# RWKV scan in residual form: values and corrections in opposite partition halves, level tiles by VectorE, keys turned by chunk

## The reference, cut to what matters

```python
def step(s, inp):
    w_t, a_t, k_t, v_t, kk_t = inp[:5]
    s = (s * w_t[:, :, None, :]
         - jnp.einsum('bhvk,bhk->bhv', s, kk_t)[..., None] * (kk_t * a_t)[:, :, None, :]
         + v_t[..., None] * k_t[:, :, None, :])
    y = jnp.einsum('bhvk,bhk->bhv', s, inp[5]) if emit else None
    return s, y
```

## Time and profile before

| what | value |
|---|---|
| median of 3 runs | 4092.16 us (4091.16, 4092.16, 4100.14) |
| span of the profiled execution | 4085.5 us, 6.7 us under the median |
| TensorE busy | 3690.0 us, 90% of the span |
| VectorE, ScalarE, GpSimd busy | 2226.9, 1064.1, 491.0 us |
| one scan stage (four of them) | 86 to 86.5 us |
| one prep stage (four of them) | 57.5 to 61.5 us |

### The profile page before, as it was taken

The page is one execution under the profiler, slowest core; times in us unless marked ns, Lnnn a source line. Parts: engine busy times, 40 slices in busy tenths (PEclk is TensorE's granted clock), DMA queues, the critical chain, the costliest instruction groups (busy, mean ns, idle before and its releaser), DMA issues. The chain is left out here.

```text
span 4085.5 us, 66177 instructions
## 1 busy us (share of the span) xinstructions
PE 3690.0 (90%) x27408; PEld 2046.7 (50%) x27408; DVE 2226.9 (55%) x3700; ACT 1064.1 (26%) x2366; POOL 491.0 (12%) x675
## 2 busy tenths in 40 slices
PE   7899999687896899999998899997697968999998
PEld 4555665476643333333334655664586533333333
DVE  3554324688756544444443554335778667655654
ACT  3442110634311111111112542113444211111121
POOL 1100000221210111111111200000232110010100
PEclk9899999688998999999999899998798989999999
DMA  7200120200276577788873000211100336999996
GB/s 264 94 1 11 60 75 0 90 3 19 70 296 234 182 267 267 268 273 273 269 254 99 32 1 11 73 56 58 33 10 13 120 133 245 336 326 335 319 332 200
DMA packets 293592, 613.14 MB, mean 150 GB/s; under 512 B 37640, under 2 KB 50184, under 8 KB 286640
## 3 DMA queue, kind: packets, MB, share of 16 engines
q1 hardware_dynamic: 272752, 542.32, 37.2%
q0 software_dynamic: 20544, 66.60, 6.3%
HBM read 561.07 MB, written 47.79 MB: 149 GB/s over the span
## 5 line engine op out<-in xcount | busy, mean ns | idle before, releaser
L3017 PE MATMUL ps<-moe_w,e_hT 128*128 128x512 f32 x1024 | 449.4, 596 | 21.5 <-issue 8.9
L3148 DVE TENSOR_TENSOR moe_w<-moe_w 128x2048 f32<-128x2048 f32 x128 | 287.2, 2286 | 200.5 <-PE ps L2947 157.2
L2917 PE MATMUL ps<-moe_w,e_xs 128*64 128x512 f32 x1536 | 348.6, 596 | 0.8 <-DVE moe_w L3148 0.8
L2917 PE MATMUL ps<-moe_w,e_xT 128*64 128x512 f32 x1536 | 340.6, 592 | 0.8 <-DVE moe_w L3148 0.8
L3017 PEld LDWEIGHTS ps<-moe_w,e_hT 128*128 128x128 f32 x1024 | 192.3, 190 | 258.4 <-issue 255.6
L3154 DVE TENSOR_TENSOR e_cb<-e_part,ps 128x512 f32<-128x512 f32 x128 | 87.9, 686 | 335.1 <-ACT e_part L3056 249.3
L2917 PEld LDWEIGHTS ps<-moe_w,e_xT 128*64 128x64 f32 x1536 | 110.7, 137 | 218.7 <-issue 218.7
L2917 PEld LDWEIGHTS ps<-moe_w,e_xs 128*64 128x64 f32 x1536 | 105.3, 137 | 193.8 <-issue 192.3
L1197 PE MATMUL ps<-M 96*128 96x512 f32 (+1 forms) x400 | 183.2, 544 | 2.9 <-PEq L748 2.1
L3056 ACT COPY e_part<-ps 128x512 f32<-128x512 f32 x96 | 56.3, 586 | 480.7 <-PE ps L2917 472.4
L1057 PE MATMUL ps<-yT,hT 128*128 128x272 f32 (+1 forms) x608 | 148.1, 399 | 1.6 <-DMA yT<-in_w_in_dram 1.6
(11 more groups left out here) (420 smaller groups left out, 7163.9 us busy)
## 6 DMA issues: line engine op xcount, KB each, us to landing
moe_w<-in_w_gate_dram SPq DMA_DIRECT2D x128, 1024.0 KB, 14.1
moe_w<-in_w_up_dram SPq DMA_DIRECT2D x128, 1024.0 KB, 14.2
moe_w<-in_w_down_dram SPq DMA_DIRECT2D x128, 1024.0 KB, 13.2
m_mod_w<-in_w_ada_dram SPq DMA_DIRECT2D x24, 1024.0 KB, 6.6
o_mod_w<-in_w_ada_dram SPq DMA_DIRECT2D x24, 1024.0 KB, 7.6
yT<-in_w_in_dram SPq DMA_DIRECT2D x6, 2048.0 KB, 7.8
r_z<-z_rows SPq DMA_DIRECT2D x20, 512.0 KB, 3.3
z_rows<-p_zo POOLq DMA_DIRECT2D x36, 256.0 KB, 2.3
```

Source lines behind the costliest of these rows:

```text
L2917: ins = nc.tensor.matmul(ps[HF * q:HF * q + HF, b, :], x[:, k], weights[q][:, k], start=(first and k == 0), stop=(k == 3), skip_group_chec ...
L3017: ins = nc.tensor.matmul(ps[:, YB + c, :], hT2[:, 4 * half + k], quarter(name, e)[:, k], start=(half == 0 and k == 0), stop=(half == 1 and ...
L3148: nc.vector.tensor_tensor(to, a, b, ALU.subtract).then_inc(*td.up())
```

## The change

What it does, by part:

- **Operands.** `BK` is laid out by chunk, with 64 columns of padding at both ends that GpSimd zeroes. `by_token` now makes, for each tile, 14 transposes that read 64 partitions each and write 64 columns, for both directions at once. A chunk's key tile holds in one partition half the keys for the correction and in the other those for the value, and the values lie in the half in which the corrections don't. ScalarE copies a tile with three instructions (10 tiles, 30 copies), two tiles deep.
- **Residual form.** `W1`, `W2`, `MV`, `U`, `Se`, and `m_v`, `w1_w2`, `decayed` are gone. The carry of a chunk is now: `carry_r` on TensorE (masked products times values plus scaled queries `KE` times state), a negated ScalarE copy to `RR`, `carry_u` on TensorE (the inverse times `RR`), two ScalarE copies of 64x64 that put the correction beside the values, `carry_s` on TensorE with matmuls that contract over all 128 partitions, and VectorE's update of `S` from PSUM in one instruction.
- **Products.** They are issued in two groups of eight for both directions; the second group waits until the first is done. Each of the matmuls signals.
- **Level tiles.** VectorE writes both levels of `NL` straight from PSUM with one instruction (`level_rows`), then `UM` with three instead of four tiles per chunk; `level_x` waits for both. GpSimd makes `KE` instead.
- **T three deep.** Block rows are written up to two steps ahead. The next step's products wait for the last level of `TS`.

The diff, cut to its core (scan, then prep):

```diff
-                def products(d, s):
-                    if s:
-                        pe.wait_ge(*we[d].at(s))
...
+                def products(s, first):
+
+                    for d in DD:
+                        if first and s:
+                            pe.wait_ge(*ts[d].at(s * NLV))
+                        elif not first:
+                            pe.wait_ge(*p0[d].at(4 * s + 4))
+                    for c in range(2):
+                        for h in range(2):
+                            for d in DD:
+                                a = d if first else 1 - d
+                                out = ps[HALF[h if a else 1 - h], LV[d] + c, 0:4 * CH].rearrange("p (b n) -> p b n", n=CH)[:, a:3 + h:2 + h - a]
+                                nc.tensor.matmul(out, BK[d][HALF[h], 2 * order[d][s] + c, a], KR[d][HALF[h], :, toks(d, s, c)], start=True, stop=True) \
+                                    .then_inc(*(p0 if first else p1)[d].up())
...
+                def carry_r(d, s, q):
+                    n, c = 2 * s + q, chunks[d][q]
+                    if q == 0:
+                        pe.wait_ge(*kd[d].at(s + 1))
+                    pe.wait_ge(*su[d].at(n + 1))
+                    for h in range(2):
+                        nc.tensor.matmul(ps[HALF[1 - h], CA[d], Rc], UM[d][HALF[h], s % 2, c, 0], values(d, s, c, h)[HALF[h]], ...)
+                    for h in range(2):
+                        ins = nc.tensor.matmul(ps[HALF[1 - h], CA[d], Rc], KE[d][HALF[h], s % 2, 0, HALF[c]], S[d][HALF[h], n % 3], ...)
+                    ins.then_inc(*rm[d].up())
...
                 def carry_s(d, s, q):
                     n, c = 2 * s + q, chunks[d][q]
                     pe.wait_ge(*ue[d].at(n + 1))
+                    for h in range(2):
+                        ins = nc.tensor.matmul(ps[HALF[h], CA[d], Pc], keys(d, s, c, h), values(d, s, c, h), start=True, stop=True)
+                    ins.then_inc(*smm[d].up())
...
                 def level_x(d, s, v):
-                    pe.wait_ge(*nl[d].at(s * NLV + v + 1))
-                    pe.wait_ge(*ts[d].at(s * (NLV + 1) + v + 1))
+                    if v == 0:
+                        pe.wait_ge(*br[d].at(s + 1))
+                        pe.wait_ge(*nl[d].at(s + 1))
+                        pe.wait_ge(*um[d].at(s + 1))
+                    else:
+                        pe.wait_ge(*ts[d].at(s * NLV + v))
...
+                def level_rows(d, s):
+                    dve.wait_ge(*p1[d].at(4 * s + 4))
+                    nc.vector.tensor_tensor(NL[d][:], ps[:, LV[d]:LV[d] + 2, 0:CH].unsqueeze(1).broadcast_to([P, NLV, 2, CH]),
+                                            R["nlev"][:, d].unsqueeze(2).broadcast_to([P, NLV, 2, CH]), ALU.mult).then_inc(*nl[d].up())
...
+                def r_out(d, s, q):
+                    n = 2 * s + q
+                    act.wait_ge(*rm[d].at(n + 1))
+                    nc.scalar.activation(RR[d][:], ps[:, CA[d], Rc], ACT.Copy, scale=-1.0).then_inc(*re[d].up())
+
+                def u_out(d, s, q):
+                    n, c = 2 * s + q, chunks[d][q]
+                    act.wait_ge(*umm[d].at(n + 1))
+                    for h in range(2):
+                        ins = nc.scalar.copy(values(d, s, c, h)[HALF[1 - h]], ps[HALF[1 - h], CA[d], Uc])
+                    ins.then_inc(*ue[d].up())
```

```diff
-            for u, (d, t) in enumerate(units):
-                act.wait_ge(*turned.at(u + 1))
-                w = len(sources(d)) * P
-                nc.scalar.copy(BT[d][:, t].rearrange("p a n -> p (a n)"), ps[:, TBANKS[u % 4], 0:w]).then_inc(*tok_out.up())
+            for t in range(NT):
+                act.wait_ge(*turned.at(t + 1))
...
+                nc.scalar.copy(to[:, 2:4], two[:, :, 6 * CH:8 * CH].unsqueeze(2).broadcast_to([P, 2, 2, P])).then_inc(*tok_all.up())
+                nc.scalar.copy(to[:, 0:2], rows_[:, :, :, CH:3 * CH]).then_inc(*tok_all.up())
+                act.wait_ge(*tok_all.at(2 * t + 2))
+                nc.scalar.copy(to[CH:P, 0], rows_[CH:P, 0, :, 0:2 * CH]).then_inc(*tok_out.up())
```

More of the change, by code:

```diff
@@ L1680, in stage_rwkv_prep, with chunked @@
     allv, lnd, small = views(True), sg("ln_done"), sg("small_in")
-    turned, tok_out, ksd = sg("transposed"), sg("rw_tok"), sg("rw_ks")
-    BT, TBANKS = R["BYTOK"], (6, 3, 7, 4)
-    units = [(d, t) for t in range(NT) for d in range(2)]
-    def sources(d):
-        return (KR[d][:, 0], BK[d][:, 0], BK[d][:, 1]) + ((M[:, 4 + p],) if d == 0 else ())
+    turned, tok_all, tok_out, ksd = sg("transposed"), sg("rw_tok_all"), sg("rw_tok"), sg("rw_ks")
+    padded = sg("rw_padded")
+    BT, TBANKS = R["BYTOK"], ((3, 4), (6, 7))
+    HALF = [slice(0, CH), slice(CH, P)]
+    def chunked(a):
+        return a[:].rearrange("p (c n) -> p c n", n=CH)
     with nc.Block() as block:
@@ L1866, in _ @@
         def _(pool):
+            for d in range(2):
+                for e in (0, 2 * T + CH):
+                    ins = nc.gpsimd.memset(R["BKp"][d][:, e:e + CH], 0.0)
+            ins.then_inc(*padded.up())
             pool.wait_ge(*ed.at(2))
@@ L1931, in carry_u @@
+                    ins.then_inc(*umm[d].up())
+                    if has_y(d, s):
+                        if q == 0 and n_y(d, s):
                             pe.wait_ge(*ye[d].at(n_y(d, s)))
-                    for h in range(2):
-                        ins = nc.tensor.matmul(ps[HALF[c], CA[d] + h, Uc], W1[d][HALF[h], HALF[c]], S[d][HALF[h], n % 3],
-                                               start=True, stop=True, skip_group_check=True)
-                    if has_y(d, s):
+                        elif q == 1:
+                            pe.wait_ge(*ym[d].at(2 * n_y(d, s) + 1))
@@ L1944, in carry_s @@
                     pe.wait_ge(*ue[d].at(n + 1))
-                    for a, right in ((2, rows(d, s, 3)), (1, U[d])):
-                        if has_y(d, s):
-                            for h in range(2):
-                                nc.tensor.matmul(ps[HALF[h], CA[d] + c, Yc], right[HALF[c], HALF[h]], UM[d][HALF[c], s % 2, h, 2 * a - 1],
-                                                 start=False, stop=(a == 1), skip_group_check=True)
-                        for h in range(2):
-                            ins = nc.tensor.matmul(ps[HALF[h], CA[d] + c, Sc], rows(d, s, a)[HALF[c], HALF[h]], right[HALF[c], HALF[h]],
-                                                   start=(a == 2 and not has_y(d, s)), stop=(a == 1), skip_group_check=True)
@@ new lines, in level_x @@
+                def level_x(d, s, v):
+                    if v == 0:
[4 more added lines that the diff above has]
+                        pe.wait_ge(*ts[d].at(s * NLV + v))
+                    for c in range(2):
+                        for h in range(2):
+                            ins = nc.tensor.matmul(ps[HALF[h], LV[d], c * CH:(c + 1) * CH], NL[d][HALF[h], v, c], TS[d][HALF[h], s % 3, 0, c],
@@ L1971, in level_x @@
                                                    start=True, stop=True)
                     ins.then_inc(*xm[d].up())
-                def m_v(d, s):
-                    pe.wait_ge(*um[d].at(s + 1))
-                    for h in range(2):
-                        for c in range(2):
-                            ins = nc.tensor.matmul(ps[HALF[c], LV[d] + 1, HALF[h]], UM[d][HALF[c], s % 2, h, 2], rows(d, s, 3)[HALF[c], HALF[h]],
-                                                   start=True, stop=True)
-                    ins.then_inc(*mv[d].up())
@@ L2008, in _ @@
                         if car:
-                            w1_w2(d, s - 1)
+                            carry_r(d, s - 1, 0)
+                    if inv:
+                        products(s, True)
+                        products(s, False)
                     for d in DD:
-                        if inv:
-                            products(d, s)
                         if car:
@@ L2024, in _ @@
                             level_t(d, s, 0)
+                    for d in DD:
+                        if car:
+                            carry_r(d, s - 1, 1)
+                    for d in DD:
+                        if inv:
+                            level_x(d, s, 1)
                         if car:
                             carry_u(d, s - 1, 1)
-                    if inv:
-                        level_x(0, s, 1)
-                    if car:
-                        carry_s(0, s - 1, 1)
@@ L2031, in _ @@
-                    if inv:
-                        level_x(1, s, 1)
-                        level_t(0, s, 1)
-                    if car:
-                        carry_s(1, s - 1, 1)
-                    if inv:
-                        level_t(1, s, 1)
+                    for d in DD:
+                        if inv:
+                            level_t(d, s, 1)
+                    for d in DD:
+                        if car:
+                            carry_s(d, s - 1, 1)
             @block.vector
@@ L2115, in _ @@
```

(11 more changed lines are left out.)

258 lines of the change are left out of this document (126 added, 132 removed).

## The result

The changed kernel takes **4134.02 us** (median of 4 runs, 4129.59 to 4139.73) against 4091.66 us before (4 runs, 4090.03 to 4100.14): a ratio of 1.0099 with a 95% interval of 1.0077 to 1.012. It is 42 us slower. The prediction said 4110, 18 slower; its range, 4056 to 4134, ended where the measured time lies. The direction held, the size did not.

A forecast was written before the change was run, and what follows sets the result against it. It took the ring of waits within a step, not TensorE's load, as the bound: +0.49 us a step, +15.2 for four scans, +3 for prep, +18 on 4085.5, plus 6.7 to the median, 4110 us; range 4056 to 4134.

The forecast's parts named there:

- First step: First step of each scan, which has no carry: about 7.0 us against 7.80 before, -0.8.
- that the clock falls in the scans I give no case of its own: Clock in the scans: a fall through more idle time got no separate case or price.
- Piece 1: Step from products to `level_x`, direction 1: 3.3 us against 2.16 before, +1.15.
- The second waits for the first: Two groups of products at the step's start, in sequence: 0.67 + 0.06 + 0.67 = 1.40 us.
- Piece 2: Step from `level_x` to the end of the addition to T: 2.42 us against 2.40 before, 0.
- Piece 3: Step from the addition to the next products: 2.68 us against 3.36, -0.68, gained from `w1_w2` and its copies.
- The last carry: Scan's end, carry alone: 5.0 us against 4.8 before, +0.2.
- Prep: Stage ahead of each scan, ended by 30 ScalarE copies: +0.8 us each, +3 for four.
- TensorE's work as the bound: Rival for the scan step: fewer TensorE records make the kernel faster, 4040 or 4060 us; chance 0.25.
- The even case: Rival: product groups or correction copies overlap, step 7.75 to 8.05 us, kernel 4087 to 4098; chance 0.13.
- The third: Rival: 16 product signals a step and draining division changes add 0.3 and 0.4 us, kernel 4135; chance 0.12.
- The signs named beforehand: Scans 89 to 91 us, steps 8.4, TensorE under 85% busy; wrong if `level_x` starts within 2.8 us of products.

The follow-up runs named there:

- experiment 1: Changed kernel plus nine unused matmuls at the end of TensorE's part of every prep stage, keeping TensorE busy: 4117.6 us, ratio 1.0059.
- experiment 7: Kernel before the change, with only NL written by VectorE from PSUM and GpSimd's two level tiles gone: 4109.9 us, ratio 1.0052.
- experiment 10: Changed kernel with seven matmuls at prep's end, products waiting by chunk, carry_r between groups, mask by chunk, fewer signals, VectorE copying one prep tile: 4078.88 us.
- experiment 4: Changed kernel with the second group of products waiting by chunk, each half for the same half of the first group: 4114.58 us, ratio 1.0052.
- experiment 5: Changed kernel with carry_r issued between the two groups of products: 4124.51 us (4 runs), again 4115.84 us (6 runs).
- experiment 11: Changed kernel without ScalarE's third copy of each tile in prep, part of the computation thereby changed: 4131.07 us, ratio 1.0096.
- experiment 2: Kernel before the change, with the last ScalarE copy of every prep done four times: 4098.64 us, ratio 1.0013.
- experiments 8: Changed kernel with matmuls at prep's end, second product group waiting by chunk, carry_r between the groups and mask by chunk: 4089.89 us, ratio 0.9989.

## Why the prediction missed the size

- **First step, "about 7.0: -0.8".** It took 8.84 to 9.54 us. At full clock it takes 7.22 (experiment 1), so the layout was nearly right and the clock was wrong. This term and "that the clock falls in the scans I give no case of its own" are one error, worth 4 x 2.05 = 8 us in the profiled spans (+5.0 for -3.2): the fall of the clock was put at nothing, and it fell at all four entries. The rows I had the earlier trace rows showed a prep stretch and a scan at different clocks; I didn't ask what TensorE would be doing in the microseconds between them, although my own working let ScalarE's end move out by 0.8 us and its last transpose not. The idle time was in the numbers.
- **Piece 1, 3.3 us; it measured 3.56.** "The second waits for the first" was priced at a signal's hop of 0.06; it is 0.32, from 0.67 to 0.99. The mask's signal before `level_x` took 0.15 for 0.06 (885.98 to 886.13). Against that `carry_r` cost nothing after the first products. VectorE's four instructions were 1.68 for 1.70. Inside the piece I had also called the loss of GpSimd's tiles a gain, read from what sat between the mask and `level_x`; experiment 7 shows that in a full step of the old order it was none. That did not enter the sum.
- **Piece 2, 2.42 us; 2.61.** A change of division was taken at 0.09. `level_x`'s last record starts at 886.13 + 0.45 - 0.22 = 886.36, the next matmul at 886.51, which is the 0.09 over the usual 0.06. The carry of both directions took 0.61 for 0.55 and `level_t` to the end of the additions 1.62 for 1.55. The Trainium skill (TensorEngine Tiling (Array Packing), Key Properties) has the array drain on such a change; the trace agrees that there is a price, and it is less than half a record.
- **Piece 3, 2.68 us; 2.58.** `w1_w2`'s copies went, as forecast, though `carry_r` ahead of the products took 0.37 for 0.18.
- **The last carry, "took 4.8".** That was misread: the earlier trace rows give 5.00 (1080.56 to 1085.28 + 0.28). The ends of the scans, one step and the last carry each, came to +3.8 for 2.8 forecast.
- **Sum.** 8.75 for 8.41: 32 intervals at +25.1 us for 15.7. With the first steps (+5.0 for -3.2) and the ends (+3.8 for 2.8) the scans gave +34.0 for 15.2. Prep was +7.8 for 3; its tail went from 1.0 to 2.2 us as TensorE sees it, 4.9 in all, and the remaining 3 are open, as are the 5 of retention. So the failed steps are two: the clock at the scans' entry, put at nothing (8 us), and the wait of the second group for the first with the smaller hops beside it, a ring of 8.41 that is 8.75 (9 us).
- **The rivals.** TensorE's work as the bound (0.25) is refuted: it is busy for 7.39 of 8.75 us, and the same work fits in 7.65 (experiment 10). The even case did not come. The third, 4135, had the right time for a wrong reason: signals cost 0.09 us a step, not 0.3, and changes of division 0.09 each.
- **The signs named beforehand.** `level_x` of direction 1 starts 3.56 us after the products, not within 2.8; TensorE's longest idle time in the step, 0.65 us, lies in front of `level_x` of direction 0 and is ended by the mask; TensorE is under 85% busy; ScalarE's second copy follows the corrections (889.44 behind 889.11 + 0.43). All these came as said, in steps 0.34 us too long; scans of 89 to 91 us did not, they are 93 to 97.

## What to carry to other kernels

Before an engine's work is moved off what looks like the path, show that the wait behind it is ended by it, in the order in which it will stand: here 0.67 us after the mask stood unchanged when GpSimd's tiles were gone, because TensorE's queue filled it, and in a step with a shorter queue the same edit freed 0.26. In a ring through an in-order engine look first at what stands ahead of the instruction that starts it; swapping two blocks was worth 0.64 us of 8.75, more than any other single edit here. And follow TensorE over the edge of a stage: a tail of a microsecond on another engine can cost more in the next stage's clock than in its own length.

## What the runs showed of the hardware

TensorE waiting for a signal of its own previous matmuls was idle for 0.24 us. With the wait split by chunk both groups ran through and the step lost 0.22 us (experiment 4). With independent matmuls put between the groups no idle time was left, but the second group started only 0.06 us earlier (0.93 for 0.99, experiment 5). Twelve signals fewer on the products were worth 0.09 us a step, some 0.0075 each.

The granted clock was 1.00 at the end of every prep of the kernels shown. It fell to 0.5 at or just ahead of the scan's first microseconds after TensorE had been idle for 1.42 (experiment 11), 2.21 (the changed kernel) or 2.51 us (experiment 2). It stayed at 1.00 through the first step in all four scans where TensorE had been idle for 0.98 us (the kernel before) or 0.30 (experiments 8 and 10). An idle time of 0.30 was not always enough: in experiment 1 it also fell behind a stretch in which TensorE was busy for 2.31 of 4.00 us, in layer 0 and not in layer 1, with the same instructions. The price depends on how long the lower level lasts and on the code that meets it: 0.2 to 1.1 us in the old first step, 1.6 to 2.3 in the new one, against 7.22 at full clock.
